# All five conditioning parts computed in the first stage, in a kernel for a mixer and mixture-of-experts layer

## What is computed

```python
mod = silu(c) @ w_ada + b_ada                    # c: one vector of 1024 per group
sh1, sc1, ga1, sh2, sc2, ga2 = split(mod, 6)     # six parts of 1024
h = rms_norm(x, g_pre1) * (1 + sc1) + sh1
u = h @ w_in                                     # 9 column groups for the heads, 2 for gates
y_ret, y_hg = retention(u), gated_recurrence(u)  # 4 heads each
merged = sigmoid(za) * (y_ret @ w_br_ret) + sigmoid(zb) * (y_hg @ w_br_hg)
x = x + ga1 * rms_norm(merged @ w_out, g_post1)
h2 = rms_norm(x, g_pre2) * (1 + sc2) + sh2
x = x + ga2 * rms_norm(mixture_of_experts(h2), g_post2)
```

## Time and profile before

| what | us |
|---|---|
| median of 3 runs | 2854.63 |
| profiled execution, its own time | 2856.68 |
| profiled execution, span of the trace | 2854.7 |
| first stage, up to its barrier | 0 to 79.7 |
| heads, up to the first work of the gates | 79.7 to 770 |
| branch gates, up to their barrier | 770 to 1001.4 |

### The profile page before, as it was taken

One profiled execution on the slowest core, in us unless ns is written; L12 is line 12 of the kernel. 1 busy time (PEld: TensorE's weight loads), 2 busy tenths in 40 slices (PEclk: granted clock), 3 DMA queues, 4 the chain that ended last, 5 costly groups with the idle time before them and its releaser, 6 DMA issues. The chain is left out here.

```text
span 2854.7 us, 48423 instructions
## 1 busy us (share of the span) xinstructions
PE 2665.3 (93%) x20566; PEld 2132.8 (75%) x20566; DVE 1786.0 (63%) x2147; ACT 1335.4 (47%) x1410; POOL 301.6 (11%) x246
## 2 busy tenths in 40 slices
PE   5999999999999988983999999999999999999993
PEld 3788888889877877862777777777777777777772
DVE  4675757767400054547777777776777777777775
ACT  5544435354211121441555555555555555555552
POOL 2010000101000011211011101110111101110110
PEclk9999999999999999995999999999999999999996
DMA  7111011011343265236788788788888888887886
GB/s 283 33 31 44 24 35 55 23 52 31 115 158 126 72 209 166 97 105 242 276 286 298 286 300 289 276 295 291 294 289 296 295 289 284 282 300 286 284 290 230
DMA packets 285775, 564.97 MB, mean 198 GB/s; under 512 B 24680, under 2 KB 91080, under 8 KB 285304
## 3 DMA queue, kind: packets, MB, share of 16 engines
q1 hardware_dynamic: 274536, 540.79, 53.2%
q0 software_dynamic: 7680, 20.98, 3.2%
q10 hardware_dynamic: 3344, 0.11, 0.1%
HBM read 514.52 MB, written 47.28 MB: 197 GB/s over the span
## 5 line engine op out<-in xcount | busy, mean ns | idle before, releaser
L2291 DVE TENSOR_TENSOR we_low<-ring,we_high 128x2048 fp32r<-128x2048 f32 x384 | 878.1, 2291 | 366.5 <-ACT we_high L2240 366.5
L2240 ACT ACTIVATE we_high<-ring 128x2048 fp32r<-128x2048 f32 x384 | 737.4, 1922 | 438.9 <-PE ps_ey L2212 279.7
L1297 PE MATMUL ps_a<-h_high,w_high 128*128 128x512 f32 (+1 forms) x696 | 252.7, 363 | 7.7 <-ACT pair L817 4.8
L1298 PE MATMUL ps_a<-h_low,w_high 128*128 128x512 f32 (+1 forms) x696 | 247.6, 356 | 0.0
L1299 PE MATMUL ps_a<-h_high,w_low 128*128 128x512 f32 (+1 forms) x696 | 247.4, 356 | 0.0
L2179 PE MATMUL ps_ep<-ring,xp 128*32 128x256 f32 x4096 | 234.3, 381 | 0.0
L2210 PE MATMUL ps_ey<-we_high,hidT_high 128*128 128x512 f32 x512 | 206.6, 403 | 0.0
L2154 PE MATMUL ps_eg<-we_high,xs_high 128*128 128x512 f32 x512 | 206.2, 403 | 0.3 <-DVE xs_low L2315 0.3
L2179 PEld LDWEIGHTS ps_ep<-ring,xp 128*32 128x32 f32 x4096 | 126.6, 110 | 99.5 <-issue 22.5
L2156 PE MATMUL ps_eu<-we_high,xs_high 128*128 128x512 f32 x512 | 200.3, 391 | 0.0
L2157 PE MATMUL ps_eu<-we_low,xs_high 128*128 128x512 f32 x512 | 200.2, 391 | 0.0
(11 more groups left out here) (308 smaller groups left out, 4976.3 us busy)
## 6 DMA issues: line engine op xcount, KB each, us to landing
ring<-in_w_gate SPq DMA_DIRECT2D x256, 512.0 KB, 9.4
ring<-in_w_up SPq DMA_DIRECT2D x256, 512.0 KB, 10.5
ring<-in_w_down SPq DMA_DIRECT2D x256, 512.0 KB, 4.4
w_raw<-in_w_in SPq DMA_DIRECT2D x52, 512.0 KB, 3.8
w_ring<-in_w_ada SPq DMA_DIRECT2D x12, 1024.0 KB, 11.1
sig_dram<-sig SPq DMA_DIRECT2D x15, 640.0 KB, 7.1
w_ada_z<-in_w_ada SPq DMA_DIRECT2D x16, 512.0 KB, 6.9
sig_g<-sig_dram SPq DMA_DIRECT2D x16, 512.0 KB, 3.8
```

The costliest lines, as they stand in the source:

```text
L1297: pe.matmul(out, w_high, x_high, start=start, stop=False)
L1298: pe.matmul(out, w_high, x_low, start=False, stop=False)
L2240: act.activation(w_high[:, s % SPLIT], t.ring[:, s % RAW], ACT.Copy).then_inc(s_high, 1)
L2291: dve.tensor_tensor(w_low[:, s % SPLIT], t.ring[:, s % RAW], w_high[:, s % SPLIT], ALU.subtract).then_inc(s_low, 1)
```

## The change

Parts 3 and 4 are computed in the first stage, in the same manner as parts 0 to 2, and are gone from the branch gates with their buffers and DMAs. The result of part 3 is kept in a bank of the heads (`t.ps_a[2]`), so the projection of the last token block waits for it to be read. `g_pre2` becomes a second vector "into columns" on ACT's queue. SP's loads stand in another order: `w_ada` pieces go ahead of x, and the last pairs of x come behind piece 7. Three pairs of x are normed ahead of the columns instead of five; the fourth pair's squares, variance and root stand around the columns and its norm behind the first tile; the fifth pair is handled in the loop.

```diff
-        PARTS = 3
+        PARTS = 5
-        ps_mod, ps_col = [ps_mod0, ps_x[2]], ps_x[3]
-        NSMALL = 8
+        ps_mod, ps_col = [ps_mod0, ps_x[2], ps_mod0, t.ps_a[2], ps_mod0], ps_x[3]
+        NSMALL = 9
...
# SyncE
+            load_w(0)
+            load_w(1)
             load_x(0)
-            load_w(0)
+            load_w(2)
+            load_w(3)
             load_x(1)
-            load_w(1)
+            load_w(4)
             load_x(2)
-            load_w(2)
+            load_w(5)
+            load_head(0)
+            load_w(6)
+            load_w(7)
             load_x(3)
-            load_w(3)
             load_x(4)
-            load_head(0)
-            for j in range(4, NJ):
+            load_w(8)
+            for j in range(9, 4 * PER):
                 load_w(j)
...
             load_head(1)
+            for j in range(4 * PER, NJ):
+                load_w(j)
             load_head(2)
...
# TensorE
-                if 2 <= tl < 2 + PER:
+                if tl >= 2:
                     mod_rows(COLS1 + tl - 2)
-                if tl in (6, 7):
-                    project(0, KC // 2 * (tl - 6), KC // 2 * (tl - 5))
-            project(1, 0, KC)
+                if tl in (7, 9):
+                    project(0, KC // 4 * (tl - 7), KC // 4 * (tl - 5))
+            mod_rows(4 * PER)
+            project(1, 0, KC // 2)
+            mod_rows(4 * PER + 1)
+            project(1, KC // 2, KC)
+            mod_rows(4 * PER + 2)
+            mod_rows(4 * PER + 3)
             project(2, 0, KC)
+            pe.wait_ge(s_modsb, PARTS)
+            pe.wait_ge(s_xact, NT)
+            pe.wait_ge(s_xdve, NT)
+            columns((3, 4))
...
# ScalarE
-                act.dma_start(pre_cols[:], t.g_pre1[0].rearrange("(c p) -> p c", p=P)).then_inc(s_small, 16)
+                for n, v in enumerate((t.g_pre1, t.g_pre2)):
+                    act.dma_start(pre_cols[:, n], v[0].rearrange("(c p) -> p c", p=P)).then_inc(s_small, 16)
...
-            for i in range(NX):
+            for i in range(3):
                 squares(i)
                 if i >= 1:
                     root(i - 1)
-            root(NX - 1)
+            root(2)
             act.wait_ge(s_first, 16)
             act.activation(t.w_high[:, 0], t.w_raw[:, 0], ACT.Copy).then_inc(s_whigh, 1)
+            squares(3)
+            root(3)
             act.wait_ge(s_cols, 1)
             for tl in range(NT):
                 evacuate(act, 2 * tl)
                 if tl >= 1:
                     high(tl - 1)
+                if tl == 0:
+                    squares(4)
+                if tl == 2:
+                    root(4)
...
# VectorE
-            for i in range(NX):
+            for i in range(3):
+                variance(i)
                 norm(i)
...
             rows(1)
-            scale_shift(t.scale1[:], t.shift1[:])
+            variance(3)
+            scale_shift(0, t.scale1[:], t.shift1[:])
             for tl in range(NT):
                 evacuate(dve, 2 * tl + 1)
                 if tl >= 1:
                     low(tl - 1)
-                if tl == 8:
+                if tl == 0:
+                    norm(3)
+                if tl == 1:
+                    variance(4)
+                if tl == 3:
+                    norm(4)
+                if tl == 6:
                     rows(2)
                     gate_row(2)
...
+            rows(3)
             low(NT - 1)
+            rows(4)
+            scale_shift(1, t.scale2[:], t.shift2[:])
...
# branch gates, TensorE
-                    if 3 <= k < 3 + KC and b != 1:
-                        ada(2 * (k - 3) + b // 2)
-                    if k == KC + 4 and b == 0:
-                        columns()
```

More of the change, by code:

```diff
@@ L125, in phase_modulation @@
         post = sb("post", [P, QW])
-        pre_cols = sb("pre_cols", [P, KC])
+        pre_cols = sb("pre_cols", [P, 2, KC])
         lb_cols = sb("lb_cols", [P, 2, HEADS])
@@ L217, in mod_rows, with columns @@
                 v, i = divmod(j, PER)
-                if i == 0 and v >= 2:
+                if i == 0 and v in (2, 4):
                     pe.wait_ge(s_modsb, v - 1)
-                mm = ada_rows(pe, ps_mod[v % 2], c_pad, w_ring[:, j % NW], i)
+                mm = ada_rows(pe, ps_mod[v], c_pad, w_ring[:, j % NW], i)
                 mm.then_inc(s_mod, 1)
-            def columns():
-                for v in range(2):
+            def columns(parts):
+                for k, v in enumerate(parts):
                     for h in range(2):
-                        o = (2 * v + h) * P
+                        o = (2 * k + h) * P
                         mm = pe.transpose(ps_col[:, o:o + P], mod[:, v, h * P:(h + 1) * P], t.ident[:])
@@ L246, in _ @@
             pe.wait_ge(s_modsb, 2)
-            columns()
+            columns((0, 1))
             def project(b, c0, c1):
@@ L250, in project @@
                 pe.wait_ge(s_hl, (o + m) // P)
+                if b == 2:
+                    pe.wait_ge(s_modsb, 4)
                 for c in range(c0, c1):
@@ L338, in rows, with scale_shift @@
                 dve.wait_ge(s_mod, PER * (v + 1))
-                dve.tensor_tensor(mod[:, v], ps_mod[v % 2][:, 0:QW], bias[:, v], ALU.add).then_inc(s_modsb, 1)
-            def scale_shift(scale, shift):
-                dve.wait_ge(s_col, 1)
+                dve.tensor_tensor(mod[:, v], ps_mod[v][:, 0:QW], bias[:, v], ALU.add).then_inc(s_modsb, 1)
+            def scale_shift(n, scale, shift):
+                dve.wait_ge(s_col, n + 1)
                 for r in range(2):
@@ L355, in gate_row, with variance @@
                 dve.tensor_tensor(post[:], mod[:, v], post[:], ALU.mult).then_inc(s_rows, 1)
-            def norm(i):
+            def variance(i):
                 v = ssum[:, 2 * i:2 * i + 2]
@@ L362, in norm @@
                 dve.reciprocal(v, v).then_inc(s_var, 1)
+            def norm(i):
                 dve.wait_ge(s_rstd, i + 1)
-                dve.tensor_scalar(x_sb[:, 2 * i], x_sb[:, 2 * i], ssum[:, 2 * i:2 * i + 1], None, ALU.mult)
-                dve.drain()
-                dve.sem_inc(s_xn, 1)
+                dve.tensor_scalar(x_sb[:, 2 * i], x_sb[:, 2 * i], ssum[:, 2 * i:2 * i + 1], None, ALU.mult).then_inc(s_xn, 1)
             dve.memset(t.ones[:], 1.0)
@@ L1324, in phase_branch_gates @@
         s_w = [sem(f"w{i}") for i in range(3)]
[L1325 to L1333, removed]
         block = ctx.enter_context(nc.Block())
@@ L1338, in _ @@
         def _(sp):
[L1339 to L1342, removed]
             def load(k):
@@ L1356, in _ @@
                 sp.dma_start(t.yT[:, m], t.yT_dram[m].rearrange("h p n -> p h n")).then_inc(t.s_branch, 16)
[L1357 to L1365, removed]
             for k in range(1, NG):
@@ L1374, in _ @@
                 sp.wait_ge(s_store[i], 16 * len([k for k in range(1, NG) if k % 3 == i]))
[L1376 to L1381, removed]
         @block.tensor
         def _(pe):
[L1385 to L1401, removed]
             for k in range(1, NG):
@@ L1414, in _ @@
                     mm.then_inc(s_mm, 1)
-                    if k == 3 and b == 0:
-                        pe.wait_ge(s_pad, 1)
-                    if 3 <= k < 3 + KC and b != 1:
-                        ada(2 * (k - 3) + b // 2)
-                    if k == KC + 4 and b == 0:
-                        columns()
         @block.scalar
@@ L1444, in _ @@
         def _(dve):
[L1445 to L1457, removed]
             for k in range(2, NG):
```

21 lines of the change are left out of this document (5 added, 16 removed).

## The result

The changed kernel takes 2848.05 us (median of 13 runs, 2846.95 to 2848.55) beside 2855.05 us (13 runs, 2851.38 to 2859.19) for the kernel before: ratio 0.9976, 95% interval 0.9968 to 0.9983, 7.0 us faster. The forecast was 2848.0 us. The profiled execution's own time is 2848.05 us, its span 2846.2 us. The sum came out better than its terms, as the traces show: the number is in part luck.

What follows compares the result with a forecast made beforehand. TensorE, busy 93% of the span, was taken as the bound, with loads and ACT limiting early parts of the first stage. Terms -17.6, +10.7 and +0.3 gave -6.6: 2850.1 us profiled, 2848.0 us median, range 2843 to 2855.

Steps and rivals of the forecast that it cites:

- The gates, -17.6 us: Branch gates: removing parts 3 and 4 brings every step to 13.78 us, saving 17.6 us.
- the columns and for waits on loads: Branch gates: 5.0 us of the 17.6 us saved, beyond 12.6 us for the sixteen pieces.
- the low end (-12.6): Branch gates: the saving if only the eight full steps come back, -12.6 us.
- The end of the stage, +10.7 us: End of first stage: added pieces, columns, scale and shift and DVE's half microsecond cost 10.7 us.
- 3.35 was taken: Tile loop: the fifth pair of x costs 2.85 us of tile slip plus 0.5 us for norms on DVE.
- the clock rival: End of first stage: the tail runs at 1.2 GHz, 18 us more, 2866 us; chance 0.06.
- The start, +0.3 us: Start of first stage: scale and shift begin at 46.8 us instead of 46.50, despite the earlier piece 7.
- 1930 packets handled by 8 us: Start, ACT's DMA queue: count from which the issue of bias was put at 18.5 us.
- the 1230 assumed: Start, ACT's DMA queue: about 1230 packets must be left unhandled when the bias issue ends, as before.
- Floats that cost nothing: Start: added floats delay neither ACT nor DVE, scale and shift 3.7 us early, 2844.0 us; chance 0.15.
- The rule of the Trainium skill: DMA queues: engines change queue after whole packets of 9 to 17 descriptors, so added floats cost about 1 us, not 10.
- Late vectors: Start: ACT is not held, DVE starts at 35.6 us, scale and shift 6.6 us late, 2854.3 us; chance 0.2.

Runs made afterwards that it cites:

- the second comparison: The changed kernel run again with no edit, beside the kernel before: 2846.82 us against 2854.67 us, ratio 0.9975.

## Why the prediction was right, and where two errors met

**The gates, -17.6 us.** Right for the trace it was read from: 231.3 - 213.3 = 18.1 us. Too large as the usual price. Over the four traces with the old gates the mean is 228.3 us, over the eight with the new ones 212.8 us: -15.5 us. The mis-sized term is the 5.0 us for "the columns and for waits on loads": it is half a microsecond of columns (the step of 14.27 us) and waits that were 4.5, 0.5, 1.7 and 0.1 us in four traces, the largest of them made longer by a lower clock behind it. Part of it I had at the low end (-12.6), none of it as something that varies.

**The end of the stage, +10.7 us.** Scale and shift to barrier is 33.4 us before and 44.0 us after: +10.6. Its parts hold one by one: pieces and columns are 7.5 us in the kernel without them, and the fifth pair is 3.2 us or somewhat more, where 3.35 was taken (2.85 on ACT and 0.5 on DVE). The tail ran without a gap and at 1.00, so the clock rival is out.

**The start, +0.3 us.** It was -1.8 us. Each link is in the trace: ACT held at `bias`, SP's queue empty, floats racing through the gap, DVE at 25 us, the fourth pair's variance last. The mis-sized term is when ACT is let go. I had 1930 packets handled by 8 us, as before; it was 1160 + 1076 = 2236, as in the kernel with the floats added (1165 + 1108). I read it as more floats queued before SP's large loads filled the engines (SP's queue moved 0.75 MB from 4 to 8 us instead of 1.10). The traces bear this out as far as they go: with `g_pre2` issued behind `g_pre1` the queue handles 2227 to 2273 packets in 8 us (five traces), and in the six where ACT issues it later or not at all, with the `lb` and `gn` vectors in their old place, 1853 to 1944. In the five, SP's first row of 4 KiB comes at 5.0 to 5.3 us, in the six at 4.3 to 4.5. What holds it is open. The 306 packets more, at 102 per us, are 3.0 us, and `bias` was indeed issued at 15.2 us instead of 18.5. At that moment some 2960 packets were through and 1280 of 4240 left, close to the 1230 assumed. The working has a slip of its own too: 24.1 + 3.0 + 2.7 is 29.8 us for piece 4, not 29.4. Measured, the load issued at 21.16 us released TensorE at 27.06, 5.9 us later. The rest follows: vector at 19.1 instead of 22.2, fourth pair at 42.0 instead of 44.

**The sum.** -15.5 + 10.6 - 1.8 = -6.7 against -7.0 measured in the 13 runs and -7.85 in the second comparison. The forecast of -6.6 rests on the right mechanisms, and on two errors of 2 us of opposite sign, which is luck. Against the profiled execution the forecast was 2850.1 us and that of the changed kernel took 2848.05; the 2.05 us then taken off for the median are what the old trace had over its own median, and the changed kernel's profiled execution lies at its median.

**The rivals.** Floats that cost nothing: excluded by the kernel before with floats added, +6.4 us. The rule of the Trainium skill that was weighed ("DMA: Bandwidth & Descriptors", section "Queues, rings and completion order") is not borne out where a queue holds single floats: from 8 to 20 us each of the two queues has 391 to 423 packets in every 4 us, in all traces but that with all vectors moved late, whose floats are through by then. Equal counts alone would also fit two queues that take turns by equal batches. The trace of the kernel before excludes that: between 9 and 18 us, in stretches of 100 ns with some ten packets of each queue, the two counts never differ by more than 2. Late vectors: real when built on purpose, 4.2 us slower than the changed kernel, and absent here because the gap in SP's queue lets the floats catch up (761 in 2 us).

## What to carry to other kernels

A vector moved one float at a time is cheap in bytes and dear in turns: beside a stream of large loads its 1024 moves cost 6 to 7 us of latency here and hold the engine that issues the DMAs behind it. It belongs behind the last load that anyone waits for. Work moved off an engine that never waits is worth its full price, but a price read in one trace may hold a stall that the next does not have: take two traces before a wait is booked as a gain.

## What was not expected of the hardware

The kernel before spreads over 10 us (2851.16 to 2861.33), the changed one over 3 us. The loads of parts 3 and 4 in the gates explain at least part: 4.4 us between four traces, and a spread of only 2 us over the four runs of the kernel with the gates alone changed. Behind TensorE's wait of 2.5 us in the old tile loop the granted clock from 70 to 80 us was 0.83 in one trace and 0.93 in the one with the floats added (where the wait ends at 77.33 us, and the clock is 0.50 from 80 to 82), both about 1.5 us later at the barrier than their start explains, and 1.00 in three others. In the gates it fell to 0.50 behind a wait of 1.99 us, too. What decides is open.
